# The first expert matrix of a decoder layer: its transposing moved into four earlier stages, and 128 tokens that fetch rows of it

## The reference, cut to what matters

```python
q = (xb @ w_q).reshape(PK_BLOCK, PK_HEADS, 2, PK_DKEY // 2)
v1, i1 = lax.top_k(s1, PK_TOPK)          # s1 = q[:, :, 0] @ sub_k1.T, s2 alike
v2, i2 = lax.top_k(s2, PK_TOPK)
...
top, pos = lax.top_k(cand, PK_TOPK)      # 16 experts for each of 8 heads
eidx = jnp.take_along_axis(cidx, pos, axis=-1)
gate = jax.nn.softmax(top, axis=-1)
act = jax.nn.gelu(jnp.einsum('thkd,td->thk', u_tab[eidx], xb), approximate=False)
return jnp.einsum('thk,thkd->td', gate * act, v_tab[eidx])
```

## Time and profile before

| | |
|---|---|
| device time, median of 3 runs | 2785.19 us (2784.17 to 2786.49) |
| the profiled execution's own time | 2789.63 us |
| its span, first to last instruction | 2787.7 us |
| mean granted TensorE clock | 0.945 |
| TensorE matmul busy | 2554.8 us (92%) |
| DVE, ACT, POOL busy | 1493.1, 801.3, 352.9 us |
| moved by DMA | 398.09 MB |

### The profile page before, as it was taken

How to read it: one execution, slowest core, us unless ns; L and a number is a source line. 1 busy time by engine, 2 the same in 40 slices (tenths; PEclk the granted TensorE clock), 3 DMA queues, 4 the chain that set the end, 5 groups by cost and what they waited for, 6 DMA issues and landing times.

```text
span 2787.7 us, 46563 instructions
## 1 busy us (share of the span) xinstructions
PE 2554.8 (92%) x19385; PEld 2379.8 (85%) x19385; DVE 1493.1 (54%) x3427; ACT 801.3 (29%) x1147; POOL 352.9 (13%) x372
## 2 busy tenths in 40 slices
PE   7976886877769999998999999999999999999997
PEld 5954666865548998786999999999999999999997
DVE  3354375426222222376677566666412468778876
ACT  3221252210112112122232344444422333333332
POOL 2000000000000000000000000000000546667520
PEclk9987898978778999998999999999999999999998
DMA  4110320001313332220333346555644789999993
GB/s 133 48 38 23 96 62 2 4 4 48 122 45 87 81 83 85 62 79 23 136 132 136 132 137 190 169 165 165 182 151 148 268 277 341 353 345 345 344 348 122
DMA packets 267010, 398.09 MB, mean 143 GB/s; under 512 B 18641, under 2 KB 192737, under 8 KB 265265
## 3 DMA queue, kind: packets, MB, share of 16 engines
q1 hardware_dynamic: 222960, 274.07, 30.5%
q0 software_dynamic: 25408, 85.38, 8.4%
q10 hardware_dynamic: 18432, 35.66, 3.5%
HBM read 325.13 MB, written 69.92 MB: 142 GB/s over the span
## 4 chain that ended last, share of the span: by engine, by line
PE 87%; DVE 9%; issue 2%; ACT 2%; DMA 0%; DVEq 0%; ACTq 0%
PE PS L988 87%; DVE arena L1545 3%; ACT arena L644 1%; DVE arena L1557 1%; PE PS L992 1%; DVE arena L1739 1%; DVE rstd L1885 1%; ACT arena L648 0%; DVE arena L1551 0%; DVE rstd L1573 0%; DVE arena L1554 0%; ACT L644 0%; DMA XT<-in_xT 0%; DVE arena L1900 0%; DMA arena<-in_memkT 0%
## 5 line engine op out<-in xcount | busy, mean ns | idle before, releaser
L2007 DVE TENSOR_TENSOR LO<-RAW,HI 128x1024 fp32r<-128x1024 f32 x256 | 314.7, 1230 | 511.9 <-ACT HI L911 504.0
L911 ACT ACTIVATE HI<-RAW 128x1024 fp32r<-128x1024 f32 x256 | 271.0, 1059 | 918.5 <-PE PS L988 891.0
L988 PE MATMUL PS<-XH,HI 128*128 128x272 f32 x2048 | 429.2, 291 | 13.8 <-DVE LO L2007 13.8
L988 PE MATMUL PS<-XH,LO 128*128 128x272 f32 x2048 | 424.9, 289 | 0.0
L988 PE MATMUL PS<-XL,HI 128*128 128x272 f32 x2048 | 423.2, 288 | 0.0
L988 PE MATMUL PS<-HT,W 128*128 128x272 f32 (+1 forms) x1536 | 376.8, 407 | 18.6 <-DVE HT L1576 12.4
L988 PEld LDWEIGHTS PS<-HT,W 128*128 128x128 f32 (+1 forms) x1536 | 293.7, 193 | 95.7 <-issue 24.0
L988 PE MATMUL PS<-WH,HI 128*128 128x416 f32 x1024 | 360.0, 352 | 0.0
L988 PE MATMUL PS<-WL,HI 128*128 128x416 f32 x1024 | 359.3, 351 | 0.0
L988 PE MATMUL PS<-WH,LO 128*128 128x416 f32 x1024 | 357.2, 349 | 0.0
L988 PEld LDWEIGHTS PS<-XH,HI 128*128 128x128 f32 x2048 | 322.5, 189 | 14.1 <-issue 14.1
(11 more groups left out here) (272 smaller groups left out, 2940.6 us busy)
## 6 DMA issues: line engine op xcount, KB each, us to landing
RAW<-in_uT SPq DMA_DIRECT2D x128, 512.0 KB
RAW<-in_vT SPq DMA_DIRECT2D x128, 512.0 KB
table_a<-AX ACTq DMA_DIRECT2D x128, 272.0 KB, 2.1
W<-in_w_in SPq DMA_DIRECT2D x58, 512.0 KB, 4.0
gate_table<-GST SPq DMA_DIRECT2D x13, 2048.0 KB, 11.3
AIN<-table_a SPq DMA_DIRECT2D x128, 208.0 KB
GQ<-gate_table SPq DMA_DIRECT2D x32, 832.0 KB
W<-in_wq SPq DMA_DIRECT2D x16, 512.0 KB, 3.9
```

The lines of the kernel that those rows point to most:

```text
L911: nc.scalar.activation(HI[:, s % NRING], RAW[:, s % NRING], ACT.Copy).then_inc(S("hi"), 1)
L988: return nc.tensor.matmul(out, lhsT, rhs, start=first, stop=last)
L2007: dve.tensor_tensor(LO_[:, s % NRING], RAW[:, s % NRING], HI[:, s % NRING].bitcast(F32), ALU.subtract).then_inc(S("lo"), 1)
```

## The change

The last 128 tokens no longer take part in `first_products`; each fetches the 128 rows of `u_tab` that it chose and DVE takes their dot products with the token. Since the matrix lies in memory transposed, it is first turned on chip: 128 tiles of 128 x 1024 are loaded by POOL, block-transposed by DVE (`turn_tile`) and stored by POOL with four DMAs into the new table `u_rows` (`turn_tiles`), whose rows have their elements in blocks of 32 in another order. `TILES` deals the tiles out: 8 in the convolutions of the mLSTM (with one buffer each for input and output), 10 in attention, 82 in the merge, 28 in the queries (two buffers each). TensorE turns the 128 tokens once (`xt`), and ACT puts them in the same order as `XTOK`. POOL gathers rows with three buffers (`GU`), DVE makes 128 dot products at slots given by `dotted_by`, and ACT applies GELU to them 32 at a time (`picked`).

`first_products` now makes 24 matmuls of 416 columns. The parts of the picking stand ten slots apart per tile instead of eight; the 104 units lie in slots 53 to 110 (46 slots with two, 12 with one). DVE makes the one-hots of a unit with two comparisons of 128 x 512, and ACT multiplies the second by the gates with four operations (`gated_hots`), in the slot in which DVE wrote them. `gather_act` is gone. The masks of the early stages lie in `CBLK`, whose space is used again for tiles and buffers; some semaphores are merged.

```diff
+NGU = 3
+TILES = {"M": (0, 8, 1), "A": (8, 10, 2), "G": (18, 82, 2), "Q": (100, 28, 2)}
...
-    return 2 + 8 * t + part
+    return 2 + 10 * t + part
...
-    return part_slot(NPT, 4) + u // 2
+    return part_slot(NPT - 1, 7) + 4 + u * 58 // (8 * NEB)
...
+def dotted_by(s):
+
+    first, even, early = part_slot(0, 7) + 5, part_slot(NPT - 1, 7) + 5, 16
+    if s < even:
+        return max(0, s - first) * early // (even - first)
+    return min(P, early + (s - even) * (P - early) // (NK - 2 - even))
...
-        table_a = nc.dram_tensor("table_a", [NK, P, T], F32, kind="Internal").ap()
+        table_a = nc.dram_tensor("table_a", [NK, P, ND], F32, kind="Internal").ap()
+        u_rows = nc.dram_tensor("u_rows", [NK, P, 4, 2 * P], F32, kind="Internal").ap()
...
+            def turn_tiles(phase):
+
+                first, n, depth = TILES[phase]
+                for i in range(first, first + n + depth):
+                    k = i - depth
+                    if k >= first:
+                        pool.wait_ge(S("tr"), k + 1)
+                        rows, turned = u_rows[k].rearrange("(b c) q x -> q c b x", b=4), tile_out[phase][(k - first) % depth]
+                        for q in range(4):
+                            pool.dma_start(rows[q], turned[32 * q:32 * q + 32].rearrange("c (b x) -> c b x", b=4)
+                                           ).then_inc(S(f"tout{k % 2}"), 16)
+                    if i < first + n:
+                        pool.dma_start(tile_in[phase][(i - first) % depth], a["uT"][:, i].rearrange("p k n -> p (k n)")
+                                       ).then_inc(S(f"tin{i % 2}"), 16)
+                for i in range(2):
+                    pool.wait_ge(S(f"tout{i}"), 64 * ((first + n + 1 - i) // 2))
...
+            turn_tiles("M")
...
             for r in range(2):
+                if r:
+                    turn_tiles("A")
...
+            turn_tiles("G")
             barrier(pool, 4)
             pool.dma_start(KSEL, a["keysT"]).then_inc(S("in1"), 16)
-
-            flat_a = table_a.rearrange("e p (t n) -> (e p t) n", n=1)
+            turn_tiles("Q")
...
+            def gather_first(j):
+
+                if j >= NGU:
+                    pool.wait_ge(S("dot"), j - NGU + 1)
+                pool.indirect_dma_start(out=GU[j % NGU][0:NGT], out_offset=None, in_=flat_u,
...
             pool.wait_ge(S("eidx"), 2)
+            for j in range(P):
+                gather_first(j)
+            pool.wait_ge(S("dot"), P)
             pool.wait_ge(S("pu"), NK)
-            for j in range(NGR):
+            for j in range(P):
                 gather_row(j)
-            for i in range(NAX):
-                pool.wait_ge(S(f"st{i}"), 16 * (NK // NAX))
-            for j in range(EB):
-                gather_act(j)
-            for j in range(P):
-                if j + EB < P:
-                    gather_act(j + EB)
-                if j + NGR < P:
-                    gather_row(j + NGR)
...
+                if i == 0:
+                    ps = take(act, "xt")
+                    turned = [ps[:, x].rearrange("t (k q r) -> t k q r", k=4, q=4) for x in range(2)]
+                    into = XTOK[:].rearrange("t (q k r) -> t k q r", q=4, k=8)
+                    f(into[:, 0:4], turned[0], ACT.Copy)
+                    out_of("xt", into[:, 4:8], turned[1], ACT.Copy)
...
-                nc.scalar.activation(halves(AX[:, e % NAX]), PS[:, e % NRING, :, 0:HALF], ACT.Gelu).then_inc(S("af"), 1)
+                nc.scalar.activation(AX[:, e % NAX], PS[:, e % NRING, 0, 0:ND], ACT.Gelu).then_inc(S("af"), 1)
...
+            def picked(g):
+
+                act.wait_ge(S("dot"), EB * (g + 1))
+                x = ACTG[0:NGT, g * EB:(g + 1) * EB]
+                nc.scalar.activation(x, x, ACT.Gelu).then_inc(S("dact"), 1)
+
+            def gated_hots(u):
+
+                act.wait_ge(S("oheq"), u + 1)
+                for x in range(4):
+                    hot = OH[:, u % NOH, 1, x]
+                    ins = nc.scalar.activation(hot, hot, ACT.Copy, scale=IT[:, 2, 4 * u + x:4 * u + x + 1])
+                ins.then_inc(S("oh1"), 1)
...
+                for u in units_at(hots_slot, s):
+                    gated_hots(u)
...
-                ps = PS[:, s % NRING]
+                ps = PS[:, s % NRING, 0, 0:ND]
                 for k in range(DT):
-                    ks = slice(k * P, (k + 1) * P)
-                    ins = exact(ps, (HI[:, s % NRING, ks], LO_[:, s % NRING, ks]), (XH[:, k, :], XL[:, k, :]),
-                                k == 0, k == DT - 1)
+                    uh, ul = [x[:, s % NRING, k * P:(k + 1) * P] for x in (HI, LO_)]
+                    mul(ps, uh, XH[:, k, :], k == 0, False)
+                    mul(ps, uh, XL[:, k, :], False, False)
+                    ins = mul(ps, ul, XH[:, k, :], False, k == DT - 1)
...
+            def turn_tile(phase):
+
+                i, (first, n, depth) = turned_tiles[0], TILES[phase]
+                assert first <= i < first + n
+                turned_tiles[0] += 1
+                dve.wait_ge(S(f"tin{i % 2}"), 16 * (i // 2 + 1))
+                k = i - depth
+                if k >= first:
+                    dve.wait_ge(S(f"tout{k % 2}"), 64 * (k // 2 + 1))
+                x, y = tile_in[phase][(i - first) % depth], tile_out[phase][(i - first) % depth]
+                dve.transpose(y.rearrange("p (b k r) -> p b k r", b=4, k=DT), x.rearrange("p (k b r) -> p b k r", k=DT, b=4)
+                              ).then_inc(S("tr"), 1)
...
+                turn_tile("M")
...
+            for _ in range(6):
+                turn_tile("A")
             for h in range(MH + 1):
                 if h < MH:
                     ps = take(dve, f"as{h}")
                     below_max(h, 4, ps.rearrange("p a (b n) -> p (a b) n", b=2))
                 if h:
                     normalise(h - 1, 4)
+                    turn_tile("A")
...
                 weight_rest(i + 1)
+                turn_tile("G")
...
                 dve.sem_inc(S("gated"), 1)
+                turn_tile("G")
                 if j:
                     tt(YM[:, n % 2, :], YM[:, n % 2, :], dst, ALU.add, S("merged") if j == 2 else None)
                 if i and j == 0:
                     merged_rest(n - 1)
+                turn_tile("G")
             merged_rest(DT - 1)
+            for _ in range(2):
+                turn_tile("G")
             for i in range(3 * DT + 1, len(SPLIT)):
                 weight_rest(i)
+                turn_tile("G")
                 n = i - 3 * DT - 1
                 full(f"x{n}", lambda x: dve.tensor_tensor(halves(XT[:, n, :]), x, halves(XT[:, n, :]), ALU.add))
+            turn_tile("G")
...
+                for _ in range(2 if i < 14 else 0):
+                    turn_tile("Q")
...
-                    a_, b_, g_ = [IT[:, r, 4 * u + x:4 * u + x + 1] for r in range(3)]
-                    dve.tensor_scalar(OH[:, u % NOH, 0, x], iota[:], a_, None, ALU.is_equal)
-                    ins = dve.tensor_scalar(OH[:, u % NOH, 1, x], iota[:], b_, g_, ALU.is_equal, ALU.mult)
-                ins.then_inc(S("oh1"), 1)
+                for i in range(2):
+                    ins = dve.tensor_tensor(OH[:, u % NOH, i], bc(iota[:], 1, 4), bc(IT[:, i, 4 * u:4 * u + 4], 2, P), ALU.is_equal)
+                ins.then_inc(S("oheq"), 1)
+
+            def dot(j):
+
+                if j == 0:
+                    dve.wait_ge(ev[SLOT["xt"]], TURN["xt"] + 1)
+                dve.wait_ge(S(f"gr{j % NGU}"), 16 * (j // NGU + 1))
+                row = GU[j % NGU][0:NGT]
+                dve.tensor_tensor_reduce(out=row, in0=row, in1=XTOK[0:NGT], scale=1.0, scalar=0.0, op0=ALU.mult, op1=ALU.add,
+                                         accum_out=ACTG[0:NGT, j:j + 1]).then_inc(S("dot"), 1)
...
+                for j in range(dotted_by(s), dotted_by(s + 1) if s < NK else 0):
+                    dot(j)
```

More of the change, by code:

```diff
@@ L66 @@
 NGR = 6
+NGU = 3
+TILES = {"M": (0, 8, 1), "A": (8, 10, 2), "G": (18, 82, 2), "Q": (100, 28, 2)}
+assert sum(n for _, n, _ in TILES.values()) == NK
 PTILES = [(ND, NGT)] + [(c, min(P, ND - c)) for c in range(0, ND, P)]
@@ L71 @@
 HALF = T // 2
+NCBLK = 2088
 AREN = 28400
@@ L191, in units_at, with dot_slot @@
     return [u for u in range(8 * NEB) if slot_of(u) == s]
+def dotted_by(s):
[3 more added lines that the diff above has]
+    return min(P, early + (s - even) * (P - early) // (NK - 2 - even))
+def dot_slot(j):
+    return min(s for s in range(NK) if dotted_by(s + 1) > j)
 def gathered_by(e):
@@ L281, in hybrid_layer @@
         EIDX = sb("EIDX", [P, 2, P], U32)
-        assert NAX * T + 3 * ND + 5 * P <= DT * T
-        sb("HTrest", [P, DT * T - NAX * T - 3 * ND - 5 * P])
+        GU = [sb(f"GU{i}", [P, D]) for i in range(NGU - 1)]
+        spare = NCBLK + DT * T - NAX * ND - 3 * ND - 5 * P - (NGU - 1) * D
+        assert spare >= 0
+        sb("spare", [P, spare])
         HI, LO_ = [sb(n, [P, NRING, DT * P], F32R) for n in ("HI", "LO")]
```

(28 more changed lines are left out.)

67 lines of the change are left out of this document (26 added, 41 removed).

## The result

The changed kernel takes 2813.52 us (median of 4 runs, 2813.08 to 2816.17), the kernel before beside it on the same chip 2785.84 us: a ratio of 1.0102, interval 1.0085 to 1.0120. It is slower by 28 us; I had forecast 21 us faster, 2764 us, in a range from 2700 to 2845. The time lies in the range, on the other side of the kernel before.

A forecast was written before the change was run, and what follows sets the result against it. PE was taken to bound the kernel, 87% of the span. First half -112, merge +78, queries +12 and token turning +1 gave -21 us: 2768.6 from 2789.63, forecast 2764 us for the median, range 2700 to 2845.

The forecast's parts named there:

- the merge: Stage where 82 tiles are turned: 4.6 us a tile plus 8 us, 385 us against 307, so 78 us more.
- the two ends: Start and end of the merge, around its 82 tiles: 8 us together.
- The tile's own sum: Merge, two buffers each: transpose, five POOL issues, landing and waits make 7.2 us, 3.6 us a tile.
- The landing: Merge: a 0.5 MB tile load lands 1.44 + 1.7 = 3.1 us after its issue.
- the merge costs more than the products bring: Rival: half-rate stores from 32 partitions make the merge 5.5 us a tile, 152 us more; total 2851 us; chance 0.2.
- The queries: Stage before the first half: 14 cycles lengthen by 8 to 18 us in all, taken as 12 us more.
- two transposes bring DVE to 9.35 us: Queries: DVE's 6.25 us search, 0.6 and 2.5 us for transposes, against a PE-bound cycle of 8.75 us.
- to 10: Queries: DVE's cycle in us where the second tile load is not back.
- The first half: Experts' first half: shorter products, plain steps 4.53 us, two-unit slots 7.8 us; 751 us, 112 us less.
- the ring: First-half unit slots: ACT and DVE wait on each other, 7.8 us; rival that it does not bind, 2693 us, chance 0.08.
- The rest: Convolutions, attention and second half cost 0 us, ends 0 and 15 for the first two; turning tokens on PE 1 us.
- the dots: DVE's dot products in first-half slots: 1.28 us each and free; at 2.28 us they would cost about 40 us.

The follow-up runs named there:

- these two kernels: The changed kernel with four stores of 4 KB pieces, rows in wrong order, from 32 neighbouring partitions (2806.45 us) or every fourth partition (2806.23 us).
- the copies first: Changed kernel with ACT's copies of finished gate units put before the gate scalings in first-half slots: 2753.03 us, ratio 0.9882 to the kernel before.

## Why the prediction was wrong

**The direction was wrong, by 48 us, and 37 of them are one term, the merge** (+114.7 where I had +78). "I take 4.6 us a tile: 82 x 4.6 = 377, and 8 us of start and end, 385 us" was the step that failed. The stage lasted 423 us, from 840 to 1263: 397 from its first transpose to its last, 4.9 a tile, then 17 us ahead of the first and 9 behind the last. So some 20 us of the shortfall are the tile and 18 the two ends, for which I had 8 in all.

The tile's own sum was 1.25 + 5 x 0.53 + 3.1 + 0.2 = 7.2 us for two. The transpose came as taken (1.25) and so did the issues (2.18 + 0.56 for five). The landing did not. 3.1 us, or 3.6 from the start of the issue, came from a lone load in attention, and for a lone load it is about right: the first tile of the merge landed after 3.9 us. With the ring running it was 5.7. POOL also takes a finished tile up only some 0.3 us after its transpose, which stood in no term. Together 2.59 + 5.77 + 1.25 + 0.04 = 9.65 us for two. I had added 1 us a tile by judgement, because "a ring of latencies over a nearly full queue does worse than either alone", without working it out. That happened to cover the landing (7.2 + 2.1 = 9.3, 4.65 a tile), and left nothing for the rest.

**Its rival, "the merge costs more than the products bring"**, is what came, at less than its price (4.9, not 5.5 us a tile). Its mechanism was only part right. Thin stores from neighbouring partitions do take the engines longer (328 against 359 GB/s, 9%, not the half that I wrote), and the Trainium skill, page "SBUF — State Buffer", section "Door 1: The DMA port swizzle", has the direction right: these two kernels differ in nothing but the partitions of a store. But spreading the partitions gave 0 us. The price was the trip.

**The queries** cost 21.5 us, not 12. The step "two transposes bring DVE to 9.35 us" was wrong in kind: with three quarters of the stores gone, the queries with all their transposes take 1.1 us more than without turning. DVE waits for the tiles there:

```profile
DVE TQ L1650 <- DMA TQ<-in_uT: 16.3, 13, 2.5
```

It is the same two-buffer trip, 5.1 us a tile, in a stage with DMA share 0.65; I had it only as "to 10" us a cycle. PE pays at the end, idle 35.34 us before its first expert product (13.8 before): the difference is the 21.5 us.

**The first half** was right: -106.8 against -112, plain steps 4.5, two-unit slots 7.67 against 7.8. The missing 5 us fit DVE's waits for gathered rows (25.5 us in 11 waits) and ACT's for the matrix (14.4 in 4), which I had put at nothing; I did not take them away, so this stays argued. That "the order leaves no way round" the ring, the ground for giving its absence 0.08, was true of the kernel as written and missed that exchanging two loops brings 60 us.

**The rest** held: convolutions and attention at nothing (first GWH 1.8 us earlier), the second half at nothing (-0.9), the dots hidden (with the copies first, slots that hold dots run at PE's own time). PE's granted clock in the merge fell from 0.99 to 0.88, with PE idle a fifth of the time; what it adds is inside the 115 us and was not separated.

**The chances**: 0.62 for faster rested on a forecast whose own range had 4.9 us a tile at its upper end, and 2790 us with it. The tile came there; the longer ends and the dearer queries, 28 us together, had no room in it.

## What to carry to other kernels

A background stream is priced by the trip of its buffers, and the landing in it must be that of a running ring, not of the lone transfer in the old trace; here that was 5.7 instead of 3.6 us. Add the pickup by the issuing engine, and the two ends of the stage, from rows too: a guess that covered only the landing turned 21 us won into 28 lost. After each edit look at what the consumer waits for: putting loads before stores moved the wait to the stores, and one more output buffer then gave 45 us. And put background tiles where the engines idle anyway: one cost 3.8 us in the merge, 0.9 in attention, and in the mLSTM 2.0 with outputs stuck behind the tiles and 0.6 without.

## What the hardware showed that was not expected

- Four stores of 128 KB from all partitions in 1 KB pieces were far worse than four from 32 partitions, for the same pieces in memory: 96 packets of 16 bytes more in each, POOL's issue 0.69 instead of 0.55 us, loads behind them landing at 7.7 instead of 5.7 us; the merge was 88 us longer.
- With stores from every fourth partition POOL's queue moved 359 instead of 328 GB/s of the time that its packets took, and the loads landed no earlier (5.6 and 5.7 us).
- The busy share of the DMA engines is no bound by itself: 0.86 to 0.89 looked full, yet a third buffer took them to 1.00 and 335 GB/s.
